# Nine places instead of six for split weight chunks, another order on GpSimd and in the gated attention

## The reference

```python
x = x + 0.5 * swiglu(rmsnorm(x, ff1_norm), ff1_w_gate, ff1_w_up, ff1_w_down)      # 1024 -> 2816 -> 1024
proj = rmsnorm(x, mix_norm) @ w_in                      # 1024 -> 7168: a (2048), q, k, v, gates (2048)
y_a = u * (W_s @ layernorm(v) + b_s)                    # gMLP; u, v = split(gelu(a))
y_b = stick_breaking_attention(q, k, v)                 # 16 heads of 64
x = x + (g_a * (y_a @ w_branch_a) + g_b * (y_b @ w_branch_b)) @ w_out
x = final_norm(x + 0.5 * swiglu(rmsnorm(x, ff2_norm), ...))
# second model: gated linear attention, swiglu, block attention, swiglu; each followed by
x = layer_norm(4**0.25 * x + y, ln_g[i, k], ln_b[i, k])
# gated linear attention, 4 heads, chunks of 64 rows:
o = rms_norm(chunk_gla(q, k, v, log_gate), norm_g) * silu(g);  y = o @ gla_w_out
```

## Time and profile before

| | us |
|---|---|
| median of three runs (1270.84 to 1273.45) | 1271.23 |
| profiled execution: its own time | 1272.64 |
| profiled execution: span of its instructions | 1270.9 |
| PE matmuls busy | 1249.0 (98% of the span), 5959 instructions |
| DVE busy | 759.8 (60%) |
| ACT busy | 604.5 (48%) |
| POOL busy | 43.2 (3%) |
| mean granted TensorE clock | 0.997 |

### The profile page before, as it was taken

The page is one execution under the profiler, slowest core; times in us unless marked ns, Lnnn a source line. Parts: engine busy times, 40 slices in busy tenths (PEclk is TensorE's granted clock), DMA queues, the critical chain, the costliest instruction groups (busy, mean ns, idle before and its releaser), DMA issues.

```text
span 1270.9 us, 15256 instructions
## 1 busy us (share of the span) xinstructions
PE 1249.0 (98%) x5959; PEld 1019.3 (80%) x5959; DVE 759.8 (60%) x1027; ACT 604.5 (48%) x784; POOL 43.2 (3%) x99
## 2 busy tenths in 40 slices
PE   8999999999999999999999999999999999999997
PEld 6888887887778888888877657888887887888886
DVE  6755546756676665555456557555557767655554
ACT  7444435556657454444345434344434554444441
POOL 2000002100000000000000010000000000000000
PEclk9999999999999999999999999999999999999999
DMA  8655555655545466565565345655564644655551
GB/s 290 194 192 190 195 165 168 243 176 149 144 153 185 153 200 209 183 196 185 168 161 164 108 128 198 213 188 185 191 197 153 197 140 125 240 190 167 193 186 52
DMA packets 119831, 226.03 MB, mean 178 GB/s; under 512 B 8120, under 2 KB 16320, under 8 KB 119760
## 3 DMA queue, kind: packets, MB, share of 16 engines
q1 hardware_dynamic: 117184, 216.10, 52.7%
q0 software_dynamic: 2560, 8.95, 2.4%
q10 hardware_dynamic: 16, 0.00, 0.0%
HBM read 223.98 MB, written 1.05 MB: 177 GB/s over the span
## 4 chain that ended last, share of the span: by engine, by line
PE 92%; DVE 5%; issue 1%; POOL 1%; ACT 1%; DMA 0%; SPq 0%; DVEq 0%; POOLq 0%; ACTq 0%
PE ps L430 28%; PE ps L435 28%; PE ps L440 28%; PE ps L378 3%; DVE wl L1467 1%; DVE X L1557 1%; DVE X L1563 1%; PE ps L759 1%; PE ps L761 1%; PE ps L590 1%; PE ps L603 1%; DVE st L1548 0%; DVE XTL L1505 0%; DVE X L1568 0%; DMA raw<-in_ff_w_gate_dram 0%
## 5 line engine op out<-in xcount | busy, mean ns | idle before, releaser
L1467 DVE TENSOR_TENSOR wl<-raw,wh 128x1024 fp32r<-128x1024 f32 x405 | 482.9, 1219 | 246.3 <-ACT wh L909 243.7
L909 ACT ACTIVATE wh<-raw 128x1024 fp32r<-128x1024 f32 x405 | 418.9, 1055 | 226.5 <-PE ps L440 202.6
L430 PE MATMUL ps<-wh,XTH 128*128 128x512 f32 (+1 forms) x1184 | 453.7, 387 | 0.0
L435 PE MATMUL ps<-wl,XTH 128*128 128x512 f32 (+1 forms) x1184 | 446.0, 380 | 3.8 <-DVE wl L1467 3.8
L440 PE MATMUL ps<-wh,XTL 128*128 128x512 f32 (+1 forms) x1184 | 348.1, 380 | 0.4 <-DVE XTL L1513 0.2
L435 PEld LDWEIGHTS ps<-wl,XTH 128*128 128x128 f32 x1184 | 223.5, 189 | 46.8 <-DVE wl L1467 6.1
L430 PEld LDWEIGHTS ps<-wh,XTH 128*128 128x128 f32 x1184 | 223.7, 189 | 45.6 <-issue 4.7
L440 PEld LDWEIGHTS ps<-wh,XTL 128*128 128x128 f32 x1184 | 216.1, 189 | 44.7 <-DVE XTL L1505 1.3
L430 PE MATMUL ps<-wh,HHf 128*128 128x512 f32 x352 | 137.8, 391 | 0.0
L435 PE MATMUL ps<-wl,HHf 128*128 128x512 f32 x352 | 137.1, 390 | 0.0
L440 PE MATMUL ps<-wh,HLf 128*128 128x512 f32 x352 | 108.4, 389 | 0.0
(11 more groups left out here) (279 smaller groups left out, 939.9 us busy)
## 6 DMA issues: line engine op xcount, KB each, us to landing
raw<-in_ffn_w_gu_dram SPq DMA_DIRECT2D x88, 512.0 KB, 4.5
raw<-in_w_in_dram SPq DMA_DIRECT2D x56, 512.0 KB, 3.7
raw<-in_ff_w_up_dram SPq DMA_DIRECT2D x44, 512.0 KB, 4.7
raw<-in_ff_w_down_dram SPq DMA_DIRECT2D x44, 512.0 KB, 4.0
raw<-in_ffn_w_down_dram SPq DMA_DIRECT2D x44, 512.0 KB, 4.3
raw<-in_ff_w_gate_dram SPq DMA_DIRECT2D x40, 512.0 KB, 4.0
raw<-in_gla_w_in_dram SPq DMA_DIRECT2D x24, 512.0 KB, 4.4
raw<-in_moba_w_in_dram SPq DMA_DIRECT2D x24, 512.0 KB, 4.4
```

What stands on the lines that cost most here:

```text
L430: e.matmul(o, lh[:, kt, rows(t)], wh[:, s, w], start=kt == 0, stop=False)
L435: e.matmul(o, lh[:, kt, rows(t)], wl[:, s, w], start=False, stop=False)
L909: e.activation(wh[:, j % NS, 0:m], raw[:, j % NR, 0:m], ACT.Copy).then_inc(S("wh"), 1)
L1467: e.tensor_tensor(wl[:, j % NS, 0:m], raw[:, j % NR, 0:m], wh[:, j % NS, 0:m].bitcast(F32), ALU.subtract).then_inc(S("wl"), 1)
```

## The change

It has four parts. **(1) Places.** Three more places for `wh` and `wl` (`wh2`, `wl2`), in memory that other tiles take from block `q0` to `wb1` and from `gv0` to `go0`; outside these stretches there are nine. A plan (`place`, `freed`) says where a chunk goes and which chunk must have been used first. **(2) When they are issued.** `lead` keeps the old distance of splits to PE; in the closing blocks `reach` issues all splits that the nine places allow, before the readout of row half 0, and fewer between the rows; in the opening blocks DVE issues no more than the block's own chunks before the readouts. **(3) POOL.** At the mixer's entrance POOL makes the first two `LNB` pairs before it waits for `U`; in the gated attention one operation pair serves both row halves. **(4) Gated attention.** `turn_o(0)` and its splits move behind the output of head 2; block `go0` has a tail of 2 chunks instead of 4.

```diff
-LEAD = NS - 1
+MORE = 3
+            wh2, wl2 = [sb(n, [P, MORE, 1024], FR, phase) for n in ("wh2", "wl2")]
...
+        held = [(first_chunk("q0"), first_chunk("wb1")), (first_chunk("gv0"), first_chunk("go0"))]
+        place, freed = [], []
+        last_use = [-NS - MORE + i for i in range(NS + MORE)]
+        for j in range(len(chunks)):
+            for begin, end in held:
+                if j == begin:
+                    last_use[NS:] = [end] * MORE
+            i = min(range(NS + MORE), key=lambda i: (last_use[i], i))
+            place.append(i)
+            freed.append(last_use[i])
+            last_use[i] = j
+        def reach(n):
+            j = max(n + 1, 0)
+            while j < len(chunks) and freed[j] <= n:
+                j += 1
+            return j - 1
+        def lead(n):
+            return min(reach(n), n + NS)
+        OPENING, CLOSING = ("f1g0", "vg0", "f2g0", "gq", "f3g0", "mq0", "f4g0"), ("f1d1", "wo1", "f2d1", "go1", "f3d1",
+                                                                                  "mo1", "f4d1")
...
-                    if j >= NS:
-                        e.wait_ge(S("used"), j - NS + 1)
+                    if freed[j] >= 0:
+                        e.wait_ge(S("used"), freed[j] + 1)
...
                 if tail:
-                    low_to(end - tail - 1 + LEAD)
+                    ahead = (reach if name in CLOSING else lead)(end - tail - 2)
+                    low_to(min(ahead, end - 1) if name in OPENING else ahead)
                     yield 0
-                    for j in range(end - tail, end - 2):
-                        low_to(j + LEAD)
+                    for j in range(end - tail, end - tail + 1 if name in CLOSING else end - 2):
+                        low_to(lead(j - 1))
...
-            for now in pe_gemm(e, "go0", GTH, GTL, wait_parts(lambda t, half: ("o", t, half)), 4):
+            for now in pe_gemm(e, "go0", GTH, GTL, wait_parts(lambda t, half: ("o", t, half)), 2):
...
-            e.wait_ge(S("wraw"), 16)
-            e.memset(wraw[0:64, :, 64:128], 0.0).then_inc(S("ws"), 1)
-            e.wait_ge(S("ws"), 1)
             for half in range(2):
+                if half == 1:
+                    e.wait_ge(S("wraw"), 16)
+                    e.memset(wraw[0:64, :, 64:128], 0.0).then_inc(S("ws"), 1)
+                    e.wait_ge(S("ws"), 1)
                 for t in range(2):
...
-                for t in range(2):
-                    i = 4 * t + h
-                    e.wait_ge(S("osq"), 2 * h + 2)
-                    recip_sqrt(OS[:, i, 1:2], OS[:, i, 0:1], 1.0 / 256, FIRST_EPS, 1).then_inc(S("orr"), 1)
-                    e.wait_ge(S("orr"), 2 * h + t + 1)
+                both = slice(2 * h, 2 * h + 2)
+                e.wait_ge(S("osq"), 2 * h + 2)
+                recip_sqrt(OS[:, both, 1], OS[:, both, 0], 1.0 / 256, FIRST_EPS, 2).then_inc(S("orr"), 1)
+                e.wait_ge(S("orr"), h + 1)
```

More of the change, by code:

```diff
@@ L118, in build @@
         with ExitStack() as phase:
+            sb("more_f2", [P, 2 * MORE, 1024], F32, phase)
             ffn_tiles["f2"] = (sb("HHf2", [P, 22, 256], FR, phase), sb("HLf2", [P, 22, 256], FR, phase),
@@ L139, in build @@
         with ExitStack() as phase:
+            sb("more_moba", [P, 2 * MORE, 1024], F32, phase)
             MQ, MK, MV = [sb(n, [P, 2, D], F32, phase) for n in ("MQ", "MK", "MV")]
@@ L284, in build @@
             aux_use(("kv", h), False)
-            if h == 2:
-                for t in range(2):
-                    aux_use(("o", t, 0), True)
-        for t in range(2):
-            aux_use(("o", t, 1), True)
+        for half in range(2):
+            for t in range(2):
+                aux_use(("o", t, half), True)
         plan_aux_x(5, ROWS)
@@ L417, in pe_products @@
             b, at, end, width, kts = blocks[name]
-            s, (_, n, _, k0) = j % NS, chunks[j]
+            _, n, _, k0 = chunks[j]
+            high, low = wh_of(j), wl_of(j)
             o = ps[:, bank_of(name, t), 0:width]
@@ L429, in pe_products @@
                     wait(e, "h", t, kt)
-                e.matmul(o, lh[:, kt, rows(t)], wh[:, s, w], start=kt == 0, stop=False)
+                e.matmul(o, lh[:, kt, rows(t)], high[:, w], start=kt == 0, stop=False)
                 if t == 0 and j < HALVES:
@@ L434, in pe_products @@
                     e.wait_ge(S("wl"), j + 1)
-                e.matmul(o, lh[:, kt, rows(t)], wl[:, s, w], start=False, stop=False)
+                e.matmul(o, lh[:, kt, rows(t)], low[:, w], start=False, stop=False)
             for c in range(n):
@@ L439, in pe_products @@
                     wait(e, "l", t, kt)
-                ins = e.matmul(o, ll[:, kt, rows(t)], wh[:, s, w], start=False, stop=kt == kts - 1)
+                ins = e.matmul(o, ll[:, kt, rows(t)], high[:, w], start=False, stop=kt == kts - 1)
             if t == 1:
@@ L773, in gates @@
                         head_out(h - 1)
+                    if h == 3:
+                        turn_o(0)
                     if h == 2 or h == 4:
@@ L926, in block @@
                 if tail:
-                    high_to(end - tail - 1 + LEAD)
+                    ahead = (reach if name in CLOSING else lead)(end - tail - 2)
+                    high_to(min(ahead, end + 1) if name in OPENING else ahead)
                     yield 0
                     for j in range(end - tail, end - 2):
-                        high_to(j + LEAD)
+                        high_to(lead(j - 1))
                     at_chunk["step"] = end - 1
@@ L1222, in gla @@
                         copy_first("gq", QG, cols(0))
-                high_to(blocks["low"][1] - 1 + LEAD)
+                high_to(lead(blocks["low"][1] - 2))
                 def split_o(half):
@@ L1318, in gla @@
                     advance(side)
-                for t in block("go0", 4):
+                for t in block("go0", 2):
                     if t == 0:
@@ L1420, in high_half @@
                 e.wait_ge(S(f"raw{j}" if h else f"raw{j}first"), 16)
-                e.activation(wh[:, j % NS, cols(h)], raw[:, j, cols(h)], ACT.Copy).then_inc(S("wh" if h else "wh_first"), 1)
+                e.activation(wh_of(j)[:, cols(h)], raw[:, j, cols(h)], ACT.Copy).then_inc(S("wh" if h else "wh_first"), 1)
             key = ("x", 1, 0, 0)
@@ L1924, in gla @@
                         copy_second("gq", QG, cols(0))
-                low_to(blocks["low"][1] - 1 + LEAD)
+                low_to(lead(blocks["low"][1] - 2))
                 e.wait_ge(S("used"), blocks["low"][2])
@@ L2036, in gla @@
                 for half in range(2):
-                    for t in block(f"go{half}", 4):
+                    for t in block(f"go{half}", 4 if half else 2):
                         if half == 0 and t == 0:
```

64 lines of the change are left out of this document (35 added, 29 removed).

## The result

The changed kernel takes 1266.99 us (median of 6 runs, 1264.82 to 1268.33) against 1271.8 for the kernel before in its 6 runs. The ratio is 0.9962, with a 95% interval of 0.9952 to 0.9972: faster by 4.8 us, where 10.2 were forecast, and above the forecast's range. The profile follows in this order: the waits as a whole, the places that the prediction did not look at, the mixer's entrance and the clock, and the closing blocks.

A forecast was written before the change was run, and what follows sets the result against it. PE, with matmuls busy 98% of the span, was taken as the bound. Gains 3.2 + 0.6 + 0.9 + 2.7 + 1.5 + 1.3 = 10.2 us off 1272.6, less 1.4 for the median, gave 1261.0 us; 8-in-10 range 1258 to 1264.

The forecast's parts named there:

- (a): Mixer's entrance: LNB no longer waits for U, leaving a shorter stop and no slow clock; gain 3.2 us, between 1.6 and 3.8.
- (b): `wo1` to `f2g0`: chunk E+3 is split ahead of row 0, ending PE's wait; gain 0.6 us, down to 0.
- (c): `f2d1` to `gq`: three splits leave the place between the rows, so row 1's residual starts earlier; gain 0.9 us.
- (e): `f3d1` to `mq0`: row 1's residual comes earlier and PE's wait for X goes; gain 1.5 us, 1.1 at least.
- (f): `mo1` to `f4g0`: row 0 is 0.5 us late, row 1 earlier; gain 1.3 us, between 0.4 and 1.7.
- (d): Gated attention, `go0`, `go1`: waits of 0.97, 0.54 and 1.26 us go, two new ones come; gain 2.7, between 1.3 and 5.2.
- both new stops: In (d): three splits ahead of GTL lose 0.8 us; five splits in `go1` make PE lose about 1.7 us.
- PE's wait for X L1610 0.4 us or less in all: Sign of being right in the changed kernel's profile: PE's waits for the normed X total at most 0.4 us.
- The clock did not fall in `go1`: Rival: the clock falls at the new stop in `go1`, costing 1.6 us, so 1262.6; chance 0.15.
- Closing blocks that give nothing: Rival: (b), (c), (e), (f) and the last parts of (d) are gone, 5 us, so 1266; chance 0.08.
- attention waits that only move: Rival: in gated attention the 0.97 and 1.26 us waits return after another instruction, 2.2 us less, so 1263.2; chance 0.12.

The follow-up runs named there:

- one split fewer: The changed kernel with one split fewer ahead of row 0 in `go0`, `go1` and `mo1`, issued behind the readout instead: 1264.6 us, ratio 0.9938.
- chunk 70: The changed kernel with chunk 70's split put ahead of the readout again in `vg0` alone: 1264.48 us, ratio 0.9938 to the kernel before.
- all mends together: The changed kernel with GpSimd waiting for four splits, `f1g0` and `vg0` splitting as before, one split fewer ahead of row 0 in `go0`, `go1`, `mo1`: 1261.64 us, ratio 0.9914.

## Why the prediction was partly wrong

**The step that failed** is the sentence "So a loss can come only from moved instructions, and I go through those." The rule in it held; going through the moved instructions left one out. The opening blocks' bound of DVE's splits moves one split in `f1g0` as well, and there no PE matmul is waiting: GpSimd is, through a count on `wl`. I had looked at moved splits by what PE wants of them, and put the start at nothing. It cost two waits of 0.62 and 1.04 us with their overlap, 2.3 us; alone 2.8 to 3.2 in time (the kernel before with that move only), and 2.3 and 3.2 came back when either side of the wait was mended.

**The second error is the term (a)**, by its clock. I counted 1.6 us for the stretch at 0.62 as if the kernel before always had it. It was there in one of two profiles of the same program. It should have entered by a chance, not whole. In the three profiles of the changed kernel PE gained, between 205 and 222 us, 3.0, 2.8 and 3.0 us against the first profile of before, and 1.3, 1.1 and 1.3 against the second (which had lost 1.7 less there: no slow stretch, and a stop of 1.79 for 2.07). So what the change gives at the entrance by waits alone is about 1.1 to 1.3 us, where the waits in (a), 2.2 less 0.6, were put at 1.6, and my 3.2 agreed with one pair of traces for a reason that is half chance. The same chance took back 1.5 us at 679 in the first profile of the changed kernel, a row that I could not have known of. The six runs of this one program spread from 1264.8 to 1268.3.

**What was right.** (b), (c), (e) and (f) to 0.1 us by the pairing, and the run without closing blocks gave back 4.8 us where these four make 4.4. In (d) both new stops came at the size worked out: 767.8 forecast and 767.93 seen for the residual, 1.7 and 1.62 for the stop; GTL's was 0.39 with 0.34 for GTH where I had 0.8. Its parts by the pairing are 2.8 up to the stop, 1.6 lost by it and 1.8 behind it, where 2.9, 1.7 and 1.5 were forecast. The rest of the stop at the entrance ended with `bbc`, as argued: 0.67 us (0.6 taken), though 0.69 to 2.06 in other executions: 2.06 where `bbc` took 7.3 us, the slowest of the bounds in (a), against 5.9 here. The 0.6 was a fortunate pick, and the stop's removal gave 1.0 in the traces.

**Slips in the working.** The sign "PE's wait for X L1610 0.4 us or less in all" contradicts step (d), whose new stop of 1.7 is a wait for just this X; the list shows 2.1. And the forecast's own range of 1259.3 to 1262.8 doesn't follow from the bounds it names: those of (a) and (d), 3.1 below and 3.0 above, give 1257.9 to 1264.0. Neither moves the forecast.

**The rivals.** The clock did not fall in `go1`: 1.00 in the window behind the stop of 1.62. Closing blocks that give nothing, and attention waits that only move, are out by the traces. None of my rivals was the case that occurred, a split whose count another engine waits for.

**The balance.** 10.2 us forecast, less 1.7 to 1.9 for the entrance as the second profile of before has it, less 2.3 for GpSimd's wait, leaves 6.0 to 6.2. The second and third profile of the changed kernel have spans of 1263.4 and 1263.8 against 1270.3 in the second one of before, 6.7 on the mean; the timed runs show 4.8 and, the second time, 5.1 by the ratio and 5.7 by the medians. The 1 to 2 us between the spans and these isn't accounted for one by one. One thing on record fits: the profiled executions set against each other here all have a mean granted clock of 0.999, and among the timed runs of one kernel those with a lower clock are the longer ones. The changed kernel's runs took 1265.7 on average at 0.999 and 1267.8 at 0.997, those of the kernel before 1271.3 and 1273.3. Stretches at half clock, which the runs without a profile don't show by place, are of that size; that they are the cause is argued, not shown. The same holds for what the runs with one edit gave beyond their place in the trace: 1.0 us with one split fewer, 2.0 with chunk 70.

**Left open.** What decides whether the clock falls behind a stop of about 2 us or behind the small matmuls, and how long the half pace at the start lasts, was not tried beyond repeating the programs.

## What to carry to other kernels

When an instruction is moved, list every wait on the semaphore that it raises, on all engines, and not only the consumer whose stall is to be mended; a wait by a bare count, such as "five splits", binds an engine to an order that nobody sees from that engine's code. How many splits fit ahead of a readout is a matter of adding durations between two times of the trace, and one too many cost its full 1.13 us in `go1`. A stretch at half clock seen in one profile belongs in a sum only with its chance; take a second profile of the same program before it is counted.

## What the runs showed of the hardware

TensorE's granted clock fell to its lower level in some executions of a program and not in others at the same place. At the mixer's entrance PE stopped for 2.07, 2.06, 1.82 and 1.79 us in four profiles, and it fell behind the first alone (the 2.06 and the 1.82 are in the runs with chunk 4's split put back and with its move alone); behind the stops of 1.62 or 1.63 in `go1`, in eight profiles, it never fell; behind the stop of 4.59 it was 0.50. It also fell where PE had not been idle: behind sixteen matmuls of two columns, 1.92 us long, to a mean of 0.59 to 0.61 over 4 us, in one of three profiles of the changed kernel and in two of its variants (GpSimd waiting for four splits, and all mends together), each time for some 1.6 us of lost time.

At the very start the matmuls ran at half pace until 10.1 and 12.1 us in two executions of the kernel before, until 12.8, 10.2 and 11.5 in three of the changed one, and until 14.6 in the run with chunk 4's split put back. The column of the granted clock showed 1.00 there. Its first record begins just where the pace doubles (10.2, 12.3, 13.1, 10.4, 11.6 and 14.9 us in the same six traces), so ahead of it the distance between matmuls tells more than the column.
